# A two-layer block on one core: the query up-projection's weights loaded by transfers of their own into their packed place, with the projections reordered

## The reference

```python
shift1, scale1, gate1, shift2, scale2, gate2 = split(c_act @ ada_w[l] + ada_b[l], 6)     # adaLN
hk = modulate(rms_norm(x, kv_norm_g), k_shift, k_scale)
c_kv, k_rope = split(hk @ w_kv_a, [256]);  c_kv = rms_norm(c_kv, kv_a_norm_g)
k_nope, v = split((c_kv @ w_kv_b).reshape(b, s, 16, 128), [64])
q = rms_norm(h @ w_dq, q_norm_g) @ w_uq           # w_uq: 256 x 1536, 16 heads of 64 nope + 32 rope columns
q_nope, q_rope = split(q.reshape(b, s, 16, 96), [64])
q_nope = rms_norm(q_nope, q_nope_norm_g)
q_rope = apply_rope(rms_norm(q_rope, q_rope_norm_g), cos, sin)
```

## Time and profile before

| | |
|---|---|
| median of 3 runs | 1273.59 us (1272.74 to 1275.84) |
| the profiled execution's own time | 1275.22 us |
| its span in the trace | 1273.4 us |
| mean granted TensorE clock | 0.993 |
| TensorE busy | 1237.6 us, 97% |
| VectorE busy | 860.0 us, 68% |
| ScalarE busy | 604.7 us, 47% |
| DMA queue of the ring (q1) | 218.63 MB, 52.9% of 16 engines |
| DMA queue of GpSimd (q0) | 26.34 MB, 6.1% of 16 engines |

### The profile page before, as it was taken

How to read it: one execution, slowest core, us unless ns; L and a number is a source line. 1 busy time by engine, 2 the same in 40 slices (tenths; PEclk the granted TensorE clock), 3 DMA queues, 4 the chain that set the end, 5 groups by cost and what they waited for, 6 DMA issues and landing times.

```text
span 1273.4 us, 25334 instructions
## 1 busy us (share of the span) xinstructions
PE 1237.6 (97%) x10911; PEld 1159.2 (91%) x10911; DVE 860.0 (68%) x1221; ACT 604.7 (47%) x790; POOL 48.2 (4%) x65
## 2 busy tenths in 40 slices
PE   6989999999999999999999999999999999999997
PEld 5768999999865599999999999999999999999997
DVE  6897899987448776668566655448369666666443
ACT  6844743433535754444455344336335546544342
POOL 4300001000000000000000000000000000000000
PEclk9999999999999999999999999999999999999998
DMA  9896589877455558554565554564554334655452
GB/s 269 262 307 225 188 291 311 295 263 238 155 205 176 188 178 285 169 194 128 189 213 174 182 171 137 181 186 127 162 167 135 138 128 154 208 170 194 151 173 74
DMA packets 219544, 246.49 MB, mean 194 GB/s; under 512 B 5840, under 2 KB 209056, under 8 KB 219456
## 3 DMA queue, kind: packets, MB, share of 16 engines
q1 hardware_dynamic: 211616, 218.63, 52.9%
q0 software_dynamic: 7488, 26.34, 6.1%
q10 hardware_dynamic: 352, 0.23, 0.1%
HBM read 244.14 MB, written 1.05 MB: 193 GB/s over the span
## 4 chain that ended last, share of the span: by engine, by line
PE 84%; DVE 5%; DMA 5%; ACT 4%; issue 2%; ACTq 0%; SPq 0%; DVEq 0%
PE PS L1768 82%; ACT PARTS L605 1%; DVE WL L1054 1%; DMA RING<-in_ada_w 1%; DVE ARENA L1076 1%; DMA RING<-in_ffn_w_gate 1%; DMA RING<-in_s_w_glu 1%; DMA RING<-in_ffn_w_down 1%; ACT ARENA L724 1%; DVE ARENA L1172 1%; DMA RING<-in_mla_w_uq 0%; DVE X L1176 0%; DMA ACC<-in_c 0%; PE PS L2103 0%; DVE PARTS L1032 0%
## 5 line engine op out<-in xcount | busy, mean ns | idle before, releaser
L1768 PE MATMUL PS<-PARTS 128*128 128x256 f32 (+3 forms) x3608 | 840.4, 283 | 0.0
L1768 PEld LDWEIGHTS PS<-PARTS 128*128 128x128 f32 (+1 forms) x3608 | 619.5, 189 | 1.4 <-issue 0.9
L1054 DVE TENSOR_TENSOR WL<-RING,PARTS 128x2048 fp32r<-128x2048 f32 (+2 forms) x189 | 387.2, 2052 | 216.6 <-ACT PARTS L605 216.1
L1768 PE MATMUL PS<-HH,WL 128*128 128x258 f32 (+3 forms) x1832 | 521.1, 284 | 2.3 <-DVE PARTS L1032 1.3
L1768 PE MATMUL PS<-HH,PARTS 128*128 128x258 f32 (+3 forms) x1832 | 519.0, 283 | 0.0
L605 ACT CAST PARTS<-RING 128x2048 fp32r<-128x2048 f32 (+2 forms) x189 | 324.1, 1717 | 284.9 <-DMA RING<-in_w_ffn_out 69.3
L1768 PEld LDWEIGHTS PS<-HH,WL 128*128 128x128 f32 (+1 forms) x1832 | 345.3, 188 | 7.0 <-issue 5.8
L1768 PEld LDWEIGHTS PS<-HH,PARTS 128*128 128x128 f32 (+1 forms) x1832 | 345.0, 188 | 0.4
L1768 PE MATMUL PS<-PARTS,WL 128*128 128x256 f32 (+1 forms) x832 | 236.8, 285 | 1.6 <-DVE WL L1054 0.8
L1768 PEld LDWEIGHTS PS<-PARTS,WL 128*128 128x128 f32 x832 | 158.2, 190 | 3.6 <-issue 2.5
L1768 PE MATMUL PS<-ARENA 128*32 128x63 f32 (+9 forms) x864 | 59.8, 274 | 4.9 <-issue 3.8
(11 more groups left out here) (346 smaller groups left out, 962.7 us busy)
## 6 DMA issues: line engine op xcount, KB each, us to landing
RING<-in_w_ffn_in SPq DMA_DIRECT2D x44, 1024.0 KB, 5.1
RING<-in_ada_w SPq DMA_DIRECT2D x32, 1024.0 KB, 8.0
RING<-in_ffn_w_gate SPq DMA_DIRECT2D x22, 1024.0 KB, 5.3
RING<-in_ffn_w_up SPq DMA_DIRECT2D x22, 1024.0 KB, 5.2
RING<-in_w_in SPq DMA_DIRECT2D x20, 1024.0 KB, 5.2
ARENA<-in_ada_w POOLq DMA_DIRECT2D x16, 1024.0 KB, 7.5
RING<-in_ffn_w_down SPq DMA_DIRECT2D x16, 768.0 KB, 4.6
RING<-in_w_ffn_out SPq DMA_DIRECT2D x16, 768.0 KB, 4.4
```

Source lines behind the costliest of these rows:

```text
L1054: V.tensor_tensor(WL[:, u % SLOTS, 0:w], RING[:, u % SLOTS, 0:w], WH[:, u % SLOTS, 0:w].bitcast(fp32), SUB)\
L1768: return nc.tensor.matmul(o, lhsT, rhs, start=start, stop=stop)
```

## The change

The unit "uq" leaves the ring's order, and all later units move up by two. GpSimd issues four transfers straight from w_uq into the packed places: the nope columns of either 128-row half of w_uq (512 KB each) ahead of adaLN transfers 10 and 12, and the rope columns (256 KB each) ahead of adaLN transfer 20, once all gate and up units are done. In memory a head's nope columns are a run of 256 bytes and its rope columns one of 128 bytes, every 384 bytes; in SBUF they land side by side. WQR moves to the place at S5_AT, where the low parts of the feed-forward's input lay. VectorE's four copies and the semaphore uq_packed go; project(0) to project(5) wait for uq_loaded, that is for all four transfers. TensorE does project(0) and project(1) directly after kv_norm, then the column products and the key's rotation; keep_warm(2, 5) goes. VectorE's key rotation and modulation come behind its second raw copy.

```diff
-        WQR, at = arena(at, 2, HEADS1 * ROPE)
+        WQR, _ = arena(S5_AT, 2, HEADS1 * ROPE)
...
-        stream("uq", w_view("mla_w_uq", 0), (0, 2), 0, 1536, 768)
...
+            UQ = A["mla_w_uq"][0].rearrange("(k p) (h c) -> p k h c", p=P, c=QK1)
             for n in range(2 * len(ADA_FFN0 + ADA_FFN1)):
                 s, h = (ADA_FFN0 + ADA_FFN1)[n // 2], n % 2
+                if n in (10, 12):
+                    k = (n - 10) // 2
+                    pool.wait_ge(S["unit_done"], AT["ffn0"] + 2)
+                    pool.dma_start(WQN[:, k, :].rearrange("p (h c) -> p h c", c=NOPE), UQ[:, k, :, 0:NOPE]).then_inc(S["uq_loaded"], 16)
                 if n == 2 * len(ADA_FFN0):
+                    pool.wait_ge(S["unit_done"], AT["ffn0"] + 2 * MT)
+                    for k in range(2):
+                        pool.dma_start(WQR[:, k, :].rearrange("p (h c) -> p h c", c=ROPE), UQ[:, k, :, NOPE:]).then_inc(S["uq_loaded"], 16)
                     pool.wait_ge(S["unit_done"], AT["wo"] + 4)
...
-            for c in range(2):
-                packed("uq", c, QK1, NOPE, ROPE, WQR, "uq_packed")
-            dve.wait_ge(S["rope_sin"], 1)
-            dve.wait_ge(S["kr_rot"], 1)
...
-            for c in range(2):
-                packed("uq", c, QK1, 0, NOPE, WQN, "uq_packed")
-
             def raw(s):
 
-                if s in HP_LAST:
-                    dve.wait_ge(S["unit_done"], AT["uq"] + HP_LAST[s])
-                else:
-                    dve.wait_ge(S["hp_proj"], HP_COUNT[s])
+                dve.wait_ge(S["hp_proj"], s + 1)
...
             for s in range(10):
                 raw(s)
+                if s == 1:
+                    dve.wait_ge(S["rope_sin"], 1)
+                    dve.wait_ge(S["kr_rot"], 1)
...
+                    dve.wait_ge(S["ada_cols"], ADA_LAST + 2)
+                    modulation(64, 72, PS[:, 6, 384:392])
...
             pe.wait_ge(S["kv_norm"], 1)
-            ada_cols(ADA_LAST)
-            ada_cols(ADA_LAST + 1)
-            mm(PS[0:ROPE, 7, 0:SEQ], rot[0:ROPE, 0:ROPE], KR[0:ROPE, 0, :], True, True).then_inc(S["kr_rot"], 1)
-
-            keep_warm(2, 5)
...
                 if s < 6:
-                    pe.wait_ge(S["uq_packed"], s + 2 if s < 2 else 3 + i // 2)
+                    pe.wait_ge(S["uq_loaded"], 64)
...
-                ins.then_inc(S["unit_done"] if s in HP_LAST else S["hp_proj"], 1)
+                ins.then_inc(S["hp_proj"], 1)
...
             for s in range(10):
                 project(s)
+                if s == 1:
+                    ada_cols(ADA_LAST)
+                    ada_cols(ADA_LAST + 1)
+                    mm(PS[0:ROPE, 7, 0:SEQ], rot[0:ROPE, 0:ROPE], KR[0:ROPE, 0, :], True, True).then_inc(S["kr_rot"], 1)
```

More of the change, by code:

```diff
@@ L359, in build @@
         w_loaded = [sem(f"w_loaded{s}") for s in range(SLOTS)]
-        names = """unit_done rope_used v_proj uq_packed kv_packed const_loaded x_loaded meta_loaded vrow_zero vrow_loaded c_loaded s5_loaded b_loaded cm_loaded pos_loaded bf_loaded
+        names = """unit_done rope_used v_proj uq_loaded kv_packed const_loaded x_loaded meta_loaded vrow_zero vrow_loaded c_loaded s5_loaded b_loaded cm_loaded pos_loaded bf_loaded
             tr_ready tr_used lam_ready lam_used bt_ready bt_used ct_ready ct_used cact_ready late_loaded cexp_ready lrow_dve lrow_act
@@ L423, in x_of @@
             return X[:, :, TALL - N_TOK[n]:TALL]
-        HP_LAST = {1: 1, 5: 2}
-        HP_COUNT = {s: s + 1 - sum(t < s for t in HP_LAST) for s in range(10)}
         HP_GAIN = ["mla_q_rope_norm_g"] * 2 + ["mla_q_nope_norm_g"] * 4 + ["k_nope_norm_g"] * 4
@@ L1457, in _ @@
             V.tensor_scalar(GQ[:, 1:2], vec("mla_q_nope_norm_g", 0), SCALE1, None, MUL)
-            for c in range(2):
-                packed("uq", c, QK1, NOPE, ROPE, WQR, "uq_packed")
-            dve.wait_ge(S["rope_sin"], 1)
-            dve.wait_ge(S["kr_rot"], 1)
-            V.tensor_tensor(KR[K, 1, :], PS[K, 7, 0:SEQ], SINQ[K, :], MUL)
-            link(V.tensor_tensor(KR[K, 2, :], KR[K, 0, :], COSQ[K, :], MUL))
-            V.tensor_tensor(KR[K, 1, :], KR[K, 1, :], KR[K, 2, :], ADD).then_inc(S["dve_step"], 1)
-            steps[0] += 1
-            dve.wait_ge(S["ada_cols"], ADA_LAST + 2)
-            modulation(64, 72, PS[:, 6, 384:392])
-            for c in range(2):
-                packed("uq", c, QK1, 0, NOPE, WQN, "uq_packed")
             def raw(s):
-                if s in HP_LAST:
-                    dve.wait_ge(S["unit_done"], AT["uq"] + HP_LAST[s])
-                else:
-                    dve.wait_ge(S["hp_proj"], HP_COUNT[s])
+                dve.wait_ge(S["hp_proj"], s + 1)
                 V.tensor_copy(RAW[s], PS[:, s % 2, :]).then_inc(S["hp_raw"], 1)
@@ L1514, in _ @@
                 raw(s)
+                if s == 1:
+                    dve.wait_ge(S["rope_sin"], 1)
+                    dve.wait_ge(S["kr_rot"], 1)
+                    V.tensor_tensor(KR[K, 1, :], PS[K, 7, 0:SEQ], SINQ[K, :], MUL)
+                    link(V.tensor_tensor(KR[K, 2, :], KR[K, 0, :], COSQ[K, :], MUL))
+                    V.tensor_tensor(KR[K, 1, :], KR[K, 1, :], KR[K, 2, :], ADD).then_inc(S["dve_step"], 1)
+                    steps[0] += 1
+                    dve.wait_ge(S["ada_cols"], ADA_LAST + 2)
+                    modulation(64, 72, PS[:, 6, 384:392])
                 if s == 2:
```

## The result

| | before | after |
|---|---|---|
| median on the same chip | 1274.02 us (1272.74 to 1275.84, 6 runs) | 1279.69 us (1278.23 to 1282.48, 6 runs) |
| ratio, 95% interval | | 1.004 (1.0028 to 1.0053) |
| profiled execution, span | 1275.22, 1273.4 us | 1280.3, 1278.5 us |

The changed kernel is 0.4% slower, 5.7 us, inside the forecast's range and 3.7 us over its point. Timed again on a second chip, against 35 executions of the kernel before (1274.4 us), it took 1276.84 us (1275.23 to 1284.37, 12 runs), ratio 1.002 (1.0006 to 1.0035). So it is slower, by 0.2 to 0.4%; the sign is settled, the size less so.

A forecast was written before the change was run, and what follows sets the result against it. The first feed-forward was taken as the bound, with TensorE, VectorE and DMA nearly full. +4.3 + 1.0 - 2.9 = +2.4 us gave 1277.6 us by the profiled execution, 1276.0 against the median; range 1270.2 to 1280.3.

The forecast's parts named there:

- the nope transfers: Term for the first feed-forward: they delay pair 8's up load, and TensorE stands still 4.3 us, ends 1.8 and 6.4.
- the middle: Term for the stretch behind kv_norm: warmers and first-copy wait gone, clock staying up, together 2.9 us less, ends 1.6 and 2.9.
- D: Lateness of the landing of pair 8's up load in the first feed-forward: taken as 4.6 us, ends 2.15 and 6.7.
- the tail: Last packets of pair 8's up load, claimed to meet adaLN transfer 11 and so land 2.4 us later still.
- the rival: Both nope transfers fall in front of one load in the feed-forward: D 6.7 us, 1278.1 us in all; chance 0.27.
- The ring's share: In the feed-forward, the ring was claimed to keep 8% of the time in which the software queue works.
- tail escapes: Rival: the up load's last packets miss adaLN transfer 11, costing 1.8 us in the feed-forward, 1273.5 in all; chance 0.15.
- The rope term: Rope transfers set back the ring's weight loads late in the first feed-forward: 1.0 us, ends 0.6 and 1.9.
- The first term: Behind kv_norm, the two keep-warm matmuls and the wait for the first copy go: 1.64 us less.
- the second: At the first projections, the granted clock stays up where it had fallen to 0.52: 1.3 us less.
- the clock gives nothing back: Rival: no clock gain at the projections, or a new fall in TensorE's standstill: +3.7 us, 1277.3 in all; chance 0.08.

The follow-up runs named there:

- Experiment 4: Kernel before plus the four transfers at the changed kernel's places, their data unused, old packing and order kept: 1278.89 us, ratio 1.0036.
- experiment 5: Changed kernel with all four transfers issued behind the first feed-forward: 1273.76 us, ratio 0.9992; timed again on another chip 1274.13 us, ratio 0.9992.
- experiment 3: Changed kernel with both nope transfers ahead of adaLN transfer 3 and both rope transfers behind the first feed-forward: 1283.8 us, ratio 1.0066.
- experiment 7: Changed kernel with the nope transfers behind the first feed-forward, the rope transfers left where the change has them: 1276.09 us, ratio 0.9997.
- experiment 1: Changed kernel with both nope transfers issued together ahead of adaLN transfer 3: 1285.65 us, ratio 1.009.
- experiment 9: Changed kernel with the same bytes at the same places, read as whole runs of 4 KB (nope) and 2 KB (rope): 1276.7 us, ratio 1.0014.
- experiment 6: Changed kernel with all four transfers behind the first feed-forward and the middle in the old order, keep_warm(2, 5) included: 1274.47 us, ratio 0.9999.
- experiment 2: Changed kernel with both rope transfers issued behind the first feed-forward, nope transfers left where the change has them: 1276.75 us, ratio 1.0022.

## Why the prediction was right and wrong

**The direction of each part was right, and that the median fell into the range is in part luck.** The transfers in the feed-forward cost more than the middle gives back. Experiment 4 shows the loss with the transfers alone; experiment 5 shows it gone with the transfers elsewhere. But the terms do not hold one by one: the nope transfers were priced at 4.3 us and cost 1.0 where the load escaped, the rope transfers at 1.0 and cost 1.4, the middle at -2.9 and gave back 1.75 at a steady clock. Falls of the clock that were in no sum made up a part of the gap.

**The mis-sized term is D, the lateness of pair 8's up load.** The prediction took 4.6 us, since the tail would meet transfer 11 but not the second nope transfer. This never occurred. The traces show two outcomes: the tail escapes (D 1.33, 1.44, 1.39, 1.78 with flat runs and 2.05 with one nope transfer), or, in one trace, it is caught by everything behind it (9.4, more than the 6.7 of the rival). The smaller values stand little over the scatter: D is 0.97 in experiment 3, with no transfer near. My reasoning that "a gap of some tenths between two software transfers is enough for the tail" failed: once the tail was caught, the ring got 69 packets in two us, and nothing that I read shows a gap for it between transfer 11 and the nope transfer issued 0.75 us behind it. The ring's share was no constant either. I took 8% of the time; in the changed kernel it got 2 packets from 214 to 217 us, while adaLN transfer 9 and the nope transfer behind it ran, and 239 from 219 to 222 us beside adaLN transfer 10, which is 22% of 360 a us. And the late load that costs is the gate load ahead of the up load, by VectorE's wait of 1.71 us over 0.48; the forecast set only the up load back. The profiled execution was the case "tail escapes", which I gave 0.15 and priced at 1.8. The wait at 262.72 is 1.37 over that of before, but the kernel before waits 1.63 there in its other trace; by the stages of all traces the price is 1.0. The wait at 213.67 (0.69) is not the transfers': experiment 5 has 0.66 there without them.

**The rope term** (+1.0, ends 0.6 and 1.9) measured 1.64 in the changed profile (1.61 + 1.19 less 0.96 and 0.20), 2.0 against experiment 5 in experiment 7, and 1.4 by the stages of all traces. It was a little too small, though not for the reason weighed then: the packets were cheaper than assumed. The software queue of the changed kernel from 299 to 300 us:

```profile
q0 software_dynamic: 58, 0.18, 73.5%
```

73.5% x 16 / 58 is 203 ns, and since these packets hold 3.1 KB on the mean, 268 ns for 4 KB. The nope packets of experiment 1 come to 76.5% x 48 / 150 = 245 ns at 3.67 KB, 273 ns for 4 KB, and both kinds with the ring silent, in experiment 5, to 89.3% x 64 / 227 = 252 ns at 3.48 KB, 296 ns for 4 KB. So 293 was near, and 350 for the 128-byte runs was too much: halving the run from 256 to 128 bytes added nothing. By the Trainium skill, DMA: Bandwidth & Descriptors (How a descriptor splits into AXI transactions, with the overhead of Why small descriptors are slow), the estimate had been 346 and 480 ns; the measured 268 to 296 contradict that, and the measurement decides. The direction of its rule on small runs holds (273 against 175 ns flat), yet experiment 9 shows that the run length isn't what the change costs.

**The middle** was forecast at -2.9 us: 1.64 for warmers and packing wait, 1.3 for the clock. With a clock that stays up the new middle takes 29.23 us, 2.84 less than the profiled 32.07. The first term measured 0.83 + 0.92 = 1.75 us (experiments 4 to 6), the second 32.07 - 30.98 = 1.1. (The four warmers that the prediction names ahead of the fall are two; each stands as two records.) But the second is no gain of the change. The kernel before, in its second trace, had no fall there (31.15), while kernels with the new middle had one in four of their ten traces, among them the changed kernel's own (30.92, 1.69 more than 29.23). I had read one execution's clock as a trait of the kernel. In the changed profile the net gain was 32.07 - 30.92 = 1.15 us. The case that the clock gives nothing back was priced rightly and given too little, 0.08.

**Outside the sum** lie falls of the clock elsewhere: 1.2 us ahead of the change, and 1.66 in the rear. With these the profile closes: 1.5 (issue) + 3.0 - 1.15 + 1.66 = 5.05 of 5.1 us. The medians' other excess fits executions in which the up load is caught (the changed kernel reached 1284.37, experiment 4 1284.58), but the kernel before itself reached 1281.65, and how often the load is caught wasn't counted, as only one or two executions of each kernel are profiled. That caught loads make the excess is argued, not shown.

**What stays open.** The fall near 955 us came in nine of ten traces of kernels with the new middle (not in experiment 5, but in its repeat), and in none of the four with the old (before twice, experiments 4 and 6). The work there is the same in all. It made 1.5 to 1.7 us of each such trace, so it is a rival for a part of the loss. I have no mechanism; and the timings don't show it, for experiment 5 is not slower than 6. Nor is it shown why a load is caught in one execution and escapes in the next. And no version beats the kernel before by more than can be told: moving the transfers off the feed-forward takes the loss away, 0.9992 twice.

## What to carry to other kernels

A transfer on a second queue is priced by what it stands in front of: the four transfers cost 2 to 3 us in the traces where the load escaped, the two nope transfers alone 9 us where it was caught or stood in front of them, and all four nothing that could be told behind the feed-forward. Where a load passes ahead of a burst by tenths of a us, as here, one trace can show the small cost and another a cost several us larger, so read the spread of the times too, and more than one trace. Ask also which of the delayed loads an engine waits for first: here it was the gate load, not the up load behind it. Before counting a clock fall as something to win back, profile the kernel more than once. And new weights that are needed late belong into the queue's idle stretch nearest to their use (here 330 to 345 us), if their place in memory is free by then.

## What the runs showed of the hardware

- Once the software queue is busy the ring gets few packets, whatever the software packets hold, but no fixed share: 69 in two us beside an adaLN transfer in experiment 2 and 239 in three us beside one in the changed kernel, 82 in two us beside short runs, against 360 in one us alone. The changed kernel's queues from 216 to 218 us:

```profile
q0 software_dynamic: 103, 0.36, 81.1%
q1 hardware_dynamic: 82, 0.08, 20.6%
```

- Runs of 128 bytes cost no more per 4 KB packet than runs of 256 (estimated 268 and 273 ns), while GpSimd's issue of a nope transfer takes 1.16 us in short runs and 0.56 flat.
- Behind a standstill of TensorE of 6.7 us the granted clock was 0.50, half of full speed, for 4 us. It also fell behind waits of 2.46 and 1.99 us, and near 955 us in a stretch in which TensorE was busy throughout. Each fall cost 1.1 to 1.7 us, which is enough to scatter single executions by several us.
